# First stage of a two-layer decoder step: the index projection goes chunk by chunk over four banks, the head weights' columns join the index keys' stationary operand, and the first transfers are issued in another order

## The reference

```
h = rms_norm(x, norm_mix[0])                       # x * rsqrt(mean(x*x) + eps) * g
q, k, v, qi, ki, wi = split(h @ attn_w_in)         # 1024 + 1024 + 1024 + 512 + 64 + 8 columns
ki = rms_norm(ki, g_kidx)
score[t, s] = sum over 8 heads of  wi[t, h] * 8**-0.5 * relu(qi[t, h, :] . ki[s, :] * 64**-0.5)
# each token attends to its 64 (prompt) or 65 (sample) best s; sample tokens also score
# 256 older index keys each, which lie in two pages of cache_kidx named by page_table
```

## Time and profile before

| | us |
|---|---|
| median of 3 runs | 1511.49 (1511.29 to 1511.58) |
| the profiled execution | 1510.78 |
| its span, first to last instruction | 1509.1 |
| TensorE busy in the span | 1495.8 (99%) |
| mean granted clock of TensorE | 0.999 of full |

### The profile page before, as it was taken

One profiled execution on the slowest core, in us unless ns is written; L12 is line 12 of the kernel. 1 busy time (PEld: TensorE's weight loads), 2 busy tenths in 40 slices (PEclk: granted clock), 3 DMA queues, 4 the chain that ended last, 5 costly groups with the idle time before them and its releaser, 6 DMA issues.

```text
span 1509.1 us, 21654 instructions
## 1 busy us (share of the span) xinstructions
PE 1495.8 (99%) x8215; PEld 1276.8 (85%) x8215; DVE 1214.4 (80%) x1106; ACT 991.3 (66%) x955; POOL 164.2 (11%) x162
## 2 busy tenths in 40 slices
PE   9999999999999999999999999999999999999998
PEld 7887789999997987888888888888888888888887
DVE  4689787666545869888888888889889888888887
ACT  4444665444445577777777777777777777777775
POOL 3554000000000036401001001001000000000100
PEclk9999999999999999999999999999999999999999
DMA  7651983345554359999999999999999999999990
GB/s 220 232 226 56 365 304 134 126 144 203 206 190 163 119 190 374 365 393 382 394 395 382 393 396 383 393 394 383 393 392 360 397 376 379 376 396 370 376 359 32
DMA packets 198855, 456.92 MB, mean 303 GB/s; under 512 B 12020, under 2 KB 15134, under 8 KB 198794
## 3 DMA queue, kind: packets, MB, share of 16 engines
q1 hardware_dynamic: 190802, 439.34, 78.5%
q0 software_dynamic: 4336, 13.15, 3.0%
q10 hardware_dynamic: 3656, 3.60, 0.8%
HBM read 444.04 MB, written 12.03 MB: 302 GB/s over the span
## 4 chain that ended last, share of the span: by engine, by line
PE 93%; DVE 4%; ACT 1%; issue 1%; DMA 0%; ACTq 0%; DVEq 0%
PE bank L2071 22%; PE bank L2591 13%; PE bank L2593 13%; PE bank L2592 13%; PE bank L2605 7%; PE bank L2607 7%; PE bank L2606 7%; PE bank L2615 2%; PE bank L2363 1%; PE bank L2264 1%; PE bank L2058 1%; DVE rt L1611 1%; PE bank L2159 1%; PE bank L2276 1%; DVE sc L1592 0%
## 5 line engine op out<-in xcount | busy, mean ns | idle before, releaser
L1856 DVE TENSOR_TENSOR wql<-ring,wqh 128x2048 fp32r<-128x2048 f32 x335 | 766.8, 2291 | 107.7 <-ACT wqh L1000 106.7
L1000 ACT ACTIVATE wqh<-ring 128x2048 fp32r<-128x2048 f32 x334 | 641.5, 1921 | 230.2 <-PE bank L2593 147.8
L2591 PE MATMUL bank<-wqh,xgh 128*128 128x512 f32 x892 | 353.6, 396 | 0.3 <-DVE wql L1856 0.3
L2592 PE MATMUL bank<-wql,xgh 128*128 128x512 f32 x896 | 349.1, 390 | 0.0
L2593 PE MATMUL bank<-wqh,xgl 128*128 128x512 f32 x892 | 348.0, 390 | 0.0
L2593 PEld LDWEIGHTS bank<-wqh,xgl 128*128 128x128 f32 x892 | 167.5, 188 | 35.9
L2591 PEld LDWEIGHTS bank<-wqh,xgh 128*128 128x128 f32 x892 | 167.5, 188 | 34.3 <-DVE wql L1856 1.1
L2592 PEld LDWEIGHTS bank<-wql,xgh 128*128 128x128 f32 x896 | 168.4, 188 | 32.9
L1000 ACT ACTIVATE wd<-ring 128x1024 fp32r<-128x1024 f32 x90 | 95.1, 1059 | 133.6 <-PE bank L2071 131.3
L2605 PE MATMUL bank<-wqh,heTh 128*128 128x512 f32 x440 | 171.4, 389 | 0.0
L2607 PE MATMUL bank<-wqh,heTl 128*128 128x512 f32 x440 | 171.2, 389 | 0.0
(11 more groups left out here) (457 smaller groups left out, 2047.8 us busy)
## 6 DMA issues: line engine op xcount, KB each, us to landing
ring<-in_moe_w_gate SPq DMA_DIRECT2D x56, 2048.0 KB, 13.8
ring<-in_moe_w_up SPq DMA_DIRECT2D x56, 2048.0 KB, 13.9
ring<-in_moe_w_down SPq DMA_DIRECT2D x56, 2048.0 KB, 13.5
ring<-in_attn_w_in SPq DMA_DIRECT2D x7, 2048.0 KB, 12.7
ring<-in_ffn_w_gate SPq DMA_DIRECT2D x5, 2048.0 KB, 11.3
ring<-in_ffn_w_up SPq DMA_DIRECT2D x5, 2048.0 KB, 7.9
ring<-in_cache_k SPq DMA_DIRECT2D x16, 512.0 KB, 7.0
ring<-in_cache_v SPq DMA_DIRECT2D x16, 512.0 KB, 6.1
```

The source lines that it names most:

```text
L1000: return nc.scalar.activation(dst, src, ACT.Copy)
L1856: return v.tensor_tensor(dst, src, head.bitcast(F32), ALU.subtract)
L2591: mm(bank, xgh[:, k, :], w_h[:, part], start=(k == 0), stop=False)
L2592: mm(bank, xgh[:, k, :], w_l[:, part], start=False, stop=False)
```

## The change

- TensorE no longer waits for all parameters before the transposes of x: one transfer of the first gain vector suffices. The other seven are issued by ScalarE after the squares, and are transposed (L2127's work) behind `wrep`.
- The transposes of x for chunks 0 to 3 go by block of tokens, as each arrives, with lone matmuls between them; all are 128 by 128, for which the sample's unused rows are zeroed first. `hE` is made from PSUM by ScalarE (even chunks) and VectorE (odd ones), and `xT` after it.
- `index_chunk`: for each chunk, all four `qi` groups, into four banks; the weights come in four transfers.
- Index keys and head weights are one stationary operand of 72 columns, in one transfer; what was doubled is now copied to both halves by ScalarE and VectorE. `wi` is made of two small transposes.
- SP: all of x first, `qi`, `kiwi`, first q tile; then four `kip` transfers ahead of each of the entries n = 3, 4, 5 and 6, behind that entry's slot wait.

The core of the diff:

```diff
     for c in range(KD):
-        A.add(("xt", c), "act")
+        of_xt(c).add(("xt", c), "act" if c % 2 == 0 else "dve")
-    SMALLW = 2 * ID + IH
+    SMALLW = ID + IH
@@ sync
-        sp.dma_start(pt_i[0:1, :], a["page_table"].rearrange("(o b) n -> o (b n)", o=1)).then_inc(pt_in, 16)
-        for m in range(1, 3):
-            src = x_prompt[P * m:P * m + P, :] if m < 2 else x_sample
-            sp.dma_start(xin[0:ROWS[m], m, :], src).then_inc(x_in[m], 16)
+        sp.dma_start(xin[:, 0, :], x_prompt[0:P, :]).then_inc(x_in[0], 16)
+        sp.dma_start(xin[:, 1, :], x_prompt[P:NP, :]).then_inc(x_in[1], 16)
+        sp.wait_ge(x_zero, 1)
+        sp.dma_start(xin[0:NS, 2, :], x_sample).then_inc(x_in[2], 16)
         for n, (name, _) in enumerate(stream):
             if held_before(n) is not None:
                 sp.wait_ge(*stream[held_before(n)][1])
-            if n == 1:
-                sp.wait_ge(par_in, 16 * 8)
-            if n == 3:
+            if 3 <= n < 7:
                 sp.wait_ge(pt_in, 16)
-                for j in range(NSEQ * PAGES):
+                for j in range(4 * n - 12, 4 * n - 8):
                     pg = sp.value_load(pt_i[0:1, j:j + 1], min_val=0, max_val=n_pool - 1)
                     sp.dma_start(kip[:, j, 0, :], a["cache_kidx"][0][bass.ds(pg, 1), :, :].rearrange("o s d -> (o s) d"))\
                       .then_inc(kip_in, 16)
...
             if name == "qi":
-                sp.dma_start(tile_cols(s, CH), cols(w_att, QI0, CH)).then_inc(got, 16)
+                for i in range(4):
+                    sp.dma_start(tile_cols(s, CH)[:, 2 * i:2 * i + 2, :], cols(w_att, QI0, CH)[:, 2 * i:2 * i + 2, :])\
+                      .then_inc(qi_in[i], 16)
             elif name == "kiwi":
-                t = tile_cols(s, SMALLW)
-                sp.dma_start(t[:, :, 0:ID], cols(w_att, KI0, ID)).then_inc(got, 16)
-                sp.dma_start(t[:, :, ID:2 * ID], cols(w_att, KI0, ID)).then_inc(got, 16)
-                sp.dma_start(t[:, :, 2 * ID:SMALLW], cols(w_att, WI0, IH)).then_inc(got, 16)
+                sp.dma_start(tile_cols(s, SMALLW), cols(w_att, KI0, SMALLW)).then_inc(got, 16)
@@ scalar
-        take_qi(0)
         act.wait_ge(*B.full(("ssq", 0)))
...
-        take_qi(2)
         act.wait_ge(sq_dve, 1)
         h_heads(h_ready, 0, hN)
-        heads_before(WRING)
+        heads_before(2)
+        take_qi(0)
+        take_qi(2)
         act.wait_ge(*B.full("ki"))
-        nc.scalar.activation(kisq[:], B.ap("ki")[:, 0:T], ACT.Square).then_inc(kisq_ok, 1)
+        for r in range(0, P, ID):
+            last = nc.scalar.activation(kisq[r:r + ID, :], B.ap("ki")[0:ID, 0:T], ACT.Square)
+        last.then_inc(kisq_ok, 1)
...
         act.wait_ge(*B.full("kissq"))
         nc.scalar.activation(rt[:], B.ap("kissq")[:, 0:T], ACT.Sqrt, scale=1.0 / P).then_inc(b_act, 1)
+        heads_before(WRING)
@@ vector
+        v.memset(ones[:], 1.0).then_inc(ones_ok, 1)
+        v.memset(xin[:, 2, :], 0.0).then_inc(x_zero, 1)
...
-        take_qi(1)
         dve.wait_ge(*B.freed(("ssq", 0)))
...
+        dve.wait_ge(hg_act, KD // 2)
         for c in range(KD):
             v.tensor_tensor(hN[:, c, :], hE[:, c, :], rt[:], ALU.mult).then_inc(h_ready, 1)
+        dve.wait_ge(zeros, 1)
+        take_qi(1)
         take_qi(3)
@@ tensor
+        pe.wait_ge(ones_ok, 1)
+        lone(6)
         pe.wait_ge(const, 1)
-        for _ in range(15):
-            mm(B.ap(("ssq", 0))[:, 0:P], ones[:], ident[:], start=True, stop=True)
-        pe.wait_ge(par_in, 16 * 8)
-        tr(A.ap("par")[:, 0:35], small[:], ident[0:35, 0:35]).then_inc(a_full, 1)
+        pe.wait_ge(mix_in, 16)
+        tr(B.ap(("xt", 1))[:, 400:400 + KD], small[0:KD, :], ident[0:KD, 0:KD]).then_inc(mix_full, 1)
+        pe.wait_ge(mix_ok0, 1)
         for m in range(3):
+            lone(m)
             pe.wait_ge(x_in[m], 16)
+            for c in (0, 1, 2, 3):
+                turn_in(c, m)
+        lone(2)
+        def index_chunk(c):
+            pe.wait_ge(*((hg_act, c // 2 + 1) if c % 2 == 0 else (hg_dve, c // 2 + 1)))
+            pe.wait_ge(qi_in[c // 2], 16)
+            for p in range(4):
+                if c == 0:
+                    A.room(pe, ("qi", p))
+                last = mm(A.ap(("qi", p))[:, 0:T], w3("qi")[:, c, P * p:P * p + P], hE[:, c, :],
+                          start=(c == 0), stop=(c == KD - 1))
+                if c == KD - 1:
+                    last.then_inc(a_full, 1)
         for c in range(KD):
+            index_chunk(c)
+            if c < 2:
+                for d in (2 * c + 4, 2 * c + 5):
+                    B.room(pe, ("xt", d))
+                    for m in range(3):
+                        turn_in(d, m)
+            if c == 4:
                 B.room(pe, ("ssq", 0))
                 pe.wait_ge(sq_dve, 1)
                 mm(B.ap(("ssq", 0))[:, 0:T], ones[:], hT[:, 0, :], start=True, stop=True).then_inc(b_full, 1)
...
         for c in range(KD):
-            last = index_weight(2, c)
-            read = mm(B.ap("ki")[:, 0:T], kw[:, c, 0:P], hE[:, c, :], start=(c == 0), stop=(c == KD - 1))
-        last.then_inc(a_full, 1)
-        read.then_inc(b_full, 1)
+            last = mm(B.ap("ki")[0:SMALLW, 0:T], kw[:, c, :], hE[:, c, :], start=(c == 0), stop=(c == KD - 1))
+        last.then_inc(b_full, 1)
         pe.wait_ge(kip2_ok, 1)
```

More of the change, by code:

```diff
@@ L335, in build @@
         ("par_in", "pt_in", "kip_in", "gm_in", "wr_in", "ws_in"))
+    mix_in, mix_full, mix_ok0, ones_ok, wi_ok = (sem(n) for n in ("mix_in", "mix_full", "mix_ok0", "ones_ok", "wi_ok"))
+    x_zero = sem("x_zero")
+    hg_act, hg_dve = sem("hg_act"), sem("hg_dve")
+    qi_in = [sem(f"qi_in{i}") for i in range(4)]
     const, zeros, chain, achain, pchain = (sem(n) for n in ("const", "zeros", "chain", "achain", "pchain"))
@@ L386, in build @@
         A.add(("qi", p), "act" if p % 2 == 0 else "dve")
-    A.add("wi", "dve")
     B.add("ki", "dve")
@@ L1026, in _ @@
         start_counters(act, y_out)
[L1027 to L1033, removed]
+        act.dma_start(small[0:8, :], a["norm_mix"][0].rearrange("(c p) -> c p", p=P)).then_inc(mix_in, 16)
+        act.dma_start(pt_i[0:1, :], a["page_table"].rearrange("(o b) n -> o (b n)", o=1)).then_inc(pt_in, 16)
+        act.wait_ge(const, 1)
+        nc.scalar.activation(rk[0:1, 3:4], epst[0:1, 0:1], ACT.Copy)
         def raw_heads(n, name, chunks, dst):
@@ L1043, in raw_heads @@
                 nc.scalar.activation(usq[:, m % 2, :], xT[:, m, :], ACT.Square).then_inc(usq_ok, 1)
[L1045 to L1051, removed]
+        act.wait_ge(mix_ok0, 1)
+        for c in range(0, KD, 2):
+            act.wait_ge(*of_xt(c).full(("xt", c)))
+            bank = of_xt(c).ap(("xt", c))[:, 0:T]
+            nc.scalar.activation(hE[:, c, :], bank, ACT.Copy, scale=gT[:, c:c + 1]).then_inc(hg_act, 1)
+            copy(xT[:, c, :], bank).then_inc(of_xt(c).free_sem(("xt", c)), 1)
+        for q in range(2):
+            for c in range(4 * q, 4 * q + 4):
+                act.wait_ge(*of_xt(c).freed(("xt", c)))
+            nc.scalar.activation(hT[:, 4 * q:4 * q + 4, :], xT[:, 4 * q:4 * q + 4, :], ACT.Square).then_inc(sq_act, 1)
+        nc.scalar.activation(rk[0:1, 3:4], epst[0:1, 0:1], ACT.Sqrt)
+        for r, w in enumerate((a["norm_ffn"][0], a["norm_mix"][1], a["norm_ffn"][1])):
+            act.dma_start(small[8 * r + 8:8 * r + 16, :], w.rearrange("(c p) -> c p", p=P)).then_inc(par_in, 16)
+        act.dma_start(small[32:33, :], a["attn_g_q"]).then_inc(par_in, 16)
+        act.dma_start(small[33:34, :], a["attn_g_k"]).then_inc(par_in, 16)
+        act.dma_start(small[34:35, 0:ID], a["attn_g_kidx"]).then_inc(par_in, 16)
+        act.dma_start(small[34:35, ID:P], a["attn_g_kidx"]).then_inc(par_in, 16)
         act.wait_ge(zeros, 1)
@@ L1491, in _ @@
         start_counters(dve, q_tail)
[L1492 to L1498, removed]
+        v.memset(ones[:], 1.0).then_inc(ones_ok, 1)
+        v.memset(xin[:, 2, :], 0.0).then_inc(x_zero, 1)
+        dve.wait_ge(mix_full, 1)
+        v.tensor_copy(gT[:, 0:KD], B.ap(("xt", 1))[:, 400:400 + KD]).then_inc(mix_ok0, 1)
+        dve.wait_ge(mix_ok0, 1)
+        for c in range(1, KD, 2):
+            dve.wait_ge(*of_xt(c).full(("xt", c)))
+            bank = of_xt(c).ap(("xt", c))[:, 0:T]
+            v.tensor_scalar(hE[:, c, :], bank, gT[:, c:c + 1], None, ALU.mult).then_inc(hg_dve, 1)
+            v.tensor_copy(xT[:, c, :], bank).then_inc(of_xt(c).free_sem(("xt", c)), 1)
         dve.wait_ge(const, 2)
@@ L1539, in _ @@
         dve.wait_ge(*B.freed("kissq"))
[L1540 to L1543, removed]
+        v.reciprocal(rt[:], rt[:]).then_inc(kiroot, 1)
         dve.wait_ge(*A.full("wrep"))
+        v.tensor_copy(gT[:, KD:35], A.ap("wrep")[:, P + KD:P + 35]).then_inc(par_ok, 1)
+        dve.wait_ge(kiroot, 1)
+        dve.wait_ge(par_ok, 1)
+        for r in range(0, P, ID):
```

(31 more changed lines are left out.)

30 lines of the change are left out of this document (8 added, 22 removed).

## The result

The changed kernel takes 1517.66 us, the median of 20 runs (1513.02 to 1518.68), beside 1512.67 for 20 of the kernel before (1510.88 to 1515.99). The prediction, 1511.4 with 1507.5 to 1513.4, was wrong. The profiled execution took 1513.34, 2.6 more than the profiled one of before (1510.78); eleven of the twenty take some 4 to 5 more still. So there are two losses to find, and the profiled execution shows only the first.

What follows compares the result with a forecast made beforehand. The prediction took late index-key pages in SP's queue to bound the first q group: -1.7 us there plus 1.6 for a fallen clock gave -0.1 on 1510.78, so 1510.7 profiled and 1511.4 median, range 1507.5 to 1513.4.

Steps and rivals of the forecast that it cites:

- TensorE's own part: First stage: index queries begin at about 9 and keys end at 31 instead of 39.4, removing 8.4 us.
- SP's order as the new bound: SP's transfer queue: last pages wait behind four 2 MB tiles, land at 36.9, copied by 38.0; -1.7 us at the mark.
- rival B: SP's queue: key pages overtake the tiles and are in at 32.9; -5.7 us, 1505.8; chance 0.12.
- The clock: TensorE's pause before the page transposes: its clock falls to half rate and restarts, costing 1.6 us (bounds 0 to 3.5).
- Rival A: TensorE's pause: the clock holds through it; 1509.8 us; chance 0.24.
- my mark: ScalarE's taking up of the first q group, at 46.80 before; all savings and costs were summed to this point.
- whatever the first q group's end moves by is what the end of the kernel moves by: From first q group to kernel end: later stages pass its shift on unchanged; -0.1 us forecast.
- the median lies 0.7 above it: Whole kernel: the median run exceeds the profiled execution by 0.7 us, so 1510.7 becomes 1511.4.
- Rival C: First stage: the clock stays low while TensorE works in short pieces between waits; +5.4 us, 1516.9; chance 0.05.

Runs made afterwards that it cites:

- e1_pages_first: Changed kernel with all sixteen page transfers issued at n = 3, ahead of the second q tile: 1510.52 us, ratio 0.998 to the kernel before.
- e11_copy_then_tails: Changed kernel, pages at n = 3, one tail before the copy, others after `hE_r`, ten routing-stage matmuls, VectorE's `hE_r` waiting for the copy: 1505.19 us, ratio 0.9945.
- e2_warm_pause: Changed kernel with 42 throwaway matmuls filling TensorE's wait for the late pages: 1510.96 us, ratio 0.9985 to the kernel before.
- e6_after_router_warm: Changed kernel with ten throwaway matmuls in the short waits of the routing stage: 1513.71 us, ratio 1.001 to the kernel before.
- e7_before_shifted: Kernel before with ten idle matmuls (2.1 us) ahead of the second q group, so the routing stage comes later: 1518.77 us, ratio 1.0029.
- e4_tails_wait: Changed kernel with all pages at n = 3 and GpSimd's weight tails held back until `hE_r` is done: 1509.43 us, ratio 0.9985 to the kernel before.
- e5_tail_ahead: Changed kernel with all pages at n = 3, GpSimd's first weight tail ahead of the page copy, the others behind `hE_r`: 1507.26 us, ratio 0.9968.
- e9_before_router_warm: Kernel before with ten throwaway matmuls in the short waits of the routing stage: 1512.44 us, ratio 0.9994 to the kernel before.

## Why the prediction was wrong

By its own steps:

- **TensorE's own part: right.** Queries from 8.75 (forecast 9), keys done at 30.19 (31). `hE_r` ran from 30.68 to 33.70, 3 us ahead of its bounds (end at 36.6 to 39.8), and so was off the path all the more.
- **SP's order as the new bound: right in kind, 1.5 us short in size.** I had the pages in at 36.9; the last landed at 38.4. The last k tile, issued at 26.90, landed 10.8 later at 37.7, where my sum had 34.7 and the short rows on top of it. The pages did not overtake (rival B): once all sixteen go ahead of the last three of these tiles, as in `e1_pages_first`, the copy comes at 31.33. The error came early: the first q tile landed at 19.3, where the sum gives 18.6 (13.0 + 5.4 + 0.2), and the second at 26.2, where it gives 24.5 with four pages before it; the two k tiles then followed at 5.8 and 5.7 us each, for 5.9. What made the 1.0 us between the first two tiles was not isolated.
- **The clock: right in kind, 0.8 to 1.0 short.** It fell and cost 2.4 to 2.6, as the stretch from the first transpose of `kip` to the first q group is 5.93 after, 3.57 in `e11_copy_then_tails` and 3.35 in `e2_warm_pause`. I had lowered half of 4.0 us to 1.6 because small instructions are not set by columns; the sixteen transposes doubled all the same, 3.68 for 1.91. Rival A, a clock that holds, is out.
- **The sum, at my mark.** ScalarE's first `sq` came at 48.93, where I forecast 46.7 and before had 46.80. The 2.2 us of error are the two terms above. Had both been sized as measured, the sum would have been -1.7 + 1.5 + 2.4 = +2.2, and the profiled execution came out at +2.6.
- **The step that failed: "whatever the first q group's end moves by is what the end of the kernel moves by."** In the profiled execution it held within 0.4 us: the mark moved by 2.1 and the end by 2.6. It failed for the median, and with it the term "the median lies 0.7 above it", which measured 4.3 (1517.66 beside 1513.34). The routing stage, 500 us later, is what the step left out: there the clock falls in some executions, at 14 us of half rate and about 5.5 us each. By their mean clocks it takes 20 of 101 executions of before and 18 of 32 of after. `e6_after_router_warm` takes the fall away and the kernel runs at 1513.7, beside 1512.4 for before with the same ten matmuls; `e7_before_shifted` brings it on in the kernel before by a delay of 2.1 us, so far as mean clocks tell. In medians: of the 5.0 us between the kernels, 1.3 are the first stage's when both are filled (from two comparisons; by their ratios, 1.0010 and 0.9994, it is 2.4, and 2.2 between the shortest groups of the two, 1513.2 and 1511.0), and the rest is how often the clock falls in the routing stage. An estimate agrees: 18 of 32 less 20 of 101, times 5.5, is 2.0 us, and 2.2 for the first stage makes 4.2, beside 3.8 between the averages of the twenty runs of each (1516.6 and 1512.8). I had looked for a fall of the clock only at the new pause, and took one profiled execution for the kernel: the three times that I had (1511.29 to 1511.58) did not show the others.
- **Rival C came nearest in time** (1516.9 for 1517.66), by coincidence, with a wrong place: its stretch of low clock through short pieces of work was real, but in the routing stage, not in the first one.
- **Not foreseen:** that moving the copy also moves the tails onto `hE_r`. The change avoids this; its two simplest repairs do not get past it, `e1_pages_first` with the tails on `hE_r`, `e4_tails_wait` with `hE_r` on the copy.

What stays open: why 2 us of shift change how often the clock falls in the routing stage. The waits before it are the same in the executions with and without a fall, and the fall is not always of one length: in the profiles of `e1_pages_first` and `e5_tail_ahead` the clock is at half for only 3.4 us (545.9 to 549.3, and 538.7 to 542.1). Open too are the runs of after near 1515.9 (6 of 32, mean clock 0.994) and of before near 1513.8 in which the clock is 0.997 or 0.998; none of after's kind was profiled, and for before's kind the fall in the first 20 us, which the profiles of `e9_before_router_warm` and `e7_before_shifted` show, is only the likely cause.

## What to carry to other kernels

When a change takes work off TensorE ahead of a wait, price what it must now wait for in the order of the transfer queue, and add the half-rate work that follows the wait; filling the wait with throwaway matmuls tells the two apart in one run. Where operations of GpSimd and VectorE that both read SBUF can meet, it pays to order them by a wait: here one such wait, 0.49 us long, turned runs at 1504.5 to 1510.4 into 1504.4 to 1505.5. And where the runs of a kernel lie in groups, look at the mean clock of each and profile one of each group before comparing medians: a stage far from the edit can decide the result.

## What the runs showed of the hardware that was not expected

- TensorE's clock fell in a stage where it was busy most of the time (3.50 of 4 us just before) and had waited no longer than 0.5 us at a time, and in other executions of the same kernel it did not fall at all.
- The granted clock does show such a fall (0.50), though at the kernel's start it reads 1.00 while the durations are those of the lower rate.
- VectorE and GpSimd, where they met at SBUF, did not take turns evenly. GpSimd's tails, 2.5 us each, let one VectorE operation of 0.44 through at a time (8 took 11.9 instead of 3.0). VectorE's eight, back to back and started 0.02 to 0.13 us sooner, kept GpSimd's one copy waiting for about all of them (3.8 to 3.9 instead of 1.03), and not for the one in flight alone.
